# Token halves in the norms, and a new order of the second block's input units

## The chip, the cores and the metric

One core of a Trainium2 chip runs the whole program in one launch. The metric is the device time in microseconds of that core, the median of the runs. Engines: TensorE (PE), VectorE (DVE), ScalarE (ACT), GpSimd (POOL) and SyncE (SP), which issues the DMAs.

## The reference

Two transformer blocks follow each other, over 512 latent tokens (x) and 256 context tokens, width 1024, all in float32. The first has four layers: pooling mixer, neighbourhood attention, gated convolution, pooling mixer, and a last norm. Each layer is

```
h = rmsnorm(x, g) * (1 + scale) + shift        # scale, shift, gate from silu(c) @ ada_w
x = x + gate * mixer(h)
```

The second block has two layers; layer 0 updates the context too, layer 1 only x:

```
q, k, v, f, u, gv = split(modulate(rms_norm(x, g1)) @ w_in)
q, k = rope(rms_norm(q)), rope(rms_norm(k))    # 8 query heads, 2 key heads of 64
mix  = concat(attention(q, k, v), fourier_mix(f),
              gelu(u) * (w_s @ rms_norm(gelu(gv)) + b_s)) @ w_out
x = x + gt1 * mix
x = x + gt2 * (relu(modulate(rms_norm(x, g2)) @ w1) ** 2 @ w2)
```

fourier_mix is the real part of a two-dimensional transform over tokens and 64 features. The norms take the mean square over the 1024 features of each token; the head norms over 64.

## The kernel before

Activations lie transposed: features on the 128 partitions, in 8 tiles k, tokens along the free axis (T = TT = 768 with the context last, or TX = 512). The work is a list of steps made by plan(); each engine walks the same list and does its share of each step, so the list's order is every engine's queue. Semaphores are counters: act_done and dve_done count finished steps, turn_mm PE's finished turns. A step's a0 and d0 are the counts before it; ACT, as a rule, waits for all DVE steps ahead of it in the list (d0).

A unit is one output tile m of a projection: 8 weight tiles, each in three passes (high by high, high by low, low by high part of the float32 split), each pass one matmul of 512 columns and, for TT, one of 256. It writes one of two PSUM turns (PS); a turn is free when the step two turns before has been read (free_turn). Weights come one unit at a time: SP loads w_raw (two buffers), ACT rounds it to w_hi (round_unit, L1028), DVE makes w_lo (split_unit); three buffers of each, and unit w + 3 is made after unit w. Chunks of the conditioning matrices (ada_chunk, L1255) hang on the units on DVE, owed chunks being given to later units (with_ada).

A norm (norm(), ahead of each layer and each MLP) follows eight "xupd" units. In each, DVE updates x, ACT squares it into T1, DVE adds it to T4. After the eighth: "nstat" (PE sums T4 over partitions, L851; ACT takes the root; DVE the reciprocal and copies it over T3), "back" (PE transposes T3 into the score bank, L859), then eight "ntile" steps: DVE scales x by it into T1 or T2 (normed), ACT makes h_hi (L1088), DVE h_lo. The two first units after it are joined: PE interleaves them, the second two tiles behind, each tile as its H tile comes. keep_warm(n) runs n matmul pairs on constants into the score bank (L762): 8 before nstat, 2 before back, 8 before the joined pair.

In the second block the input units are, in order, sk (keys, TT), sq 0 to 3 (queries), v (TT), sf (Fourier inputs), su (gate), sgv (gate values). After the first half of a unit's tiles the previous unit's head norm stands in PE's list: "hnorm" (sums of squares, L867), keep_warm(2), "back", "rope" (a permutation, L871), then DVE and ACT finish q or k. After the last unit: "four1" (first transform, L973), the last gate value's hnorm, "gtrans" (transposes, L958), "spgate" (spatial gate, L965), "gsplit", each on its turn; then scores and "four2" (second transform, L982), whose tables DC and DS are loaded over the H tiles once the last input unit is done, and the softmax stages.

## Time and profile before

| | us |
|---|---|
| median of 3 runs (2890.43 to 2904.68) | 2893.8 |
| the profiled execution | 2895.74 |
| its span | 2893.9 |

Mean granted TensorE clock 0.975. From the page, busy time by engine and the clock in 40 slices (digits are tenths; a busy PE can be running dummies or waiting inside its pipeline):

```profile
PE 2757.8 (95%) x14298; PEld 2298.9 (79%) x14298; DVE 1696.1 (59%) x2615; ACT 937.7 (32%) x1432; POOL 156.1 (5%) x84
...
PEclk8999999999999999989999999999999999999999
```

Slices of 72 us are too coarse for the stages in question; the stage windows and timelines below cut the span where the step list does. Six norms are at 313, 802, 1045, 1657, 2215 and 2523 us; the second block's layers begin at 1258 and 2228 us.

### The profile page before, as it was taken

The numbers are of one execution on the slowest core, as the hardware profiler recorded it, in microseconds if no ns is written. First come the engines' busy times: TensorE is split into PE (matmuls) and PEld (weight loads), VectorE is DVE, ScalarE is ACT, GpSimd is POOL, SyncE is SP. The second block draws the span as 40 slices with busy tenths as digits, with TensorE's granted clock in tenths as the row PEclk, the third lists the DMA queues.
The fourth block names the chain that finished last, engine by engine and source line by source line (L and its number), as shares of the span: only waits on it lengthen the run. The fifth ranks groups of instructions, "written<-read, shape, count | busy, mean of one in ns | idle before, by whom it ended". The sixth has DMA issues, their size and how long they took to land. (4 is left out here: it accounts for less than half of the span.)

```text
span 2893.9 us, 36598 instructions
## 1 busy us (share of the span) xinstructions
PE 2757.8 (95%) x14298; PEld 2298.9 (79%) x14298; DVE 1696.1 (59%) x2615; ACT 937.7 (32%) x1432; POOL 156.1 (5%) x84
## 2 busy tenths in 40 slices
PE   7998999999999999989899999999999999999999
PEld 7887778888877877767677888888887768778887
DVE  4986666666577878765556664444235446454333
ACT  2322344444232233232355231313122345333222
POOL 0000000000000000000055000000000016100000
PEclk8999999999999999989999999999999999999999
DMA  5252334443345635322200323332112110122232
GB/s 215 72 172 97 108 123 143 138 136 134 109 155 181 195 106 171 118 78 83 93 1 1 110 95 130 118 124 70 62 59 63 55 63 1 59 80 95 95 95 95
DMA packets 88539, 296.32 MB, mean 102 GB/s; under 512 B 10288, under 2 KB 13360, under 8 KB 87856
## 3 DMA queue, kind: packets, MB, share of 16 engines
q1 hardware_dynamic: 88368, 293.98, 30.7%
q8 instruction: 114, 1.87, 0.3%
q14 instruction: 57, 0.47, 0.1%
HBM read 291.85 MB, written 2.10 MB: 102 GB/s over the span
## 5 line engine op out<-in xcount | busy, mean ns | idle before, releaser
L770 PE MATMUL turns<-h_hi,w_hi 128*128 128x512 f32 (+1 forms) x2480 | 788.2, 367 | 25.2 <-DVE h_lo L1244 13.5
L770 PE MATMUL turns<-h_hi,w_lo 128*128 128x512 f32 (+1 forms) x2480 | 773.1, 361 | 0.0
L770 PE MATMUL turns<-h_lo,w_hi 128*128 128x512 f32 (+1 forms) x2480 | 770.4, 360 | 0.0
L770 PEld LDWEIGHTS turns<-h_hi,w_hi 128*128 128x128 f32 x2480 | 418.6, 190 | 119.6 <-DVE h_lo L1244 27.8
L770 PEld LDWEIGHTS turns<-h_hi,w_lo 128*128 128x128 f32 x2480 | 416.1, 189 | 72.5
L770 PEld LDWEIGHTS turns<-h_lo,w_hi 128*128 128x128 f32 x2480 | 415.3, 189 | 71.1 <-issue 1.0
L1028 ACT ACTIVATE w_hi<-w_raw 128x1024 fp32r<-128x1024 f32 x300 | 315.4, 1051 | 373.8 <-PE turns L770 352.7
L1241 DVE TENSOR_TENSOR w_lo<-w_raw,w_hi 128x1024 fp32r<-128x1024 f32 x300 | 366.7, 1223 | 118.1 <-ACT w_hi L1028 117.7
L724 POOL TENSOR_SCALAR tmp<-tmp,softmax_stats 128x768 f32<-128x768 f32 (+1 forms) x80 | 155.9, 1951 | 2317.5 <-DVE softmax_stats L1477 2317.2
L1244 DVE SCALAR_TENSOR_TENSOR x_lat<-turns,modulation,x_lat 128x512 f32<-128x512 f32 x112 | 84.1, 750 | 317.5 <-PE turns L770 317.5
L770 PE MATMUL turns<-m_hi,w_lo 128*128 128x512 f32 (+1 forms) x768 | 232.9, 358 | 0.0
L770 PE MATMUL turns<-m_hi,w_hi 128*128 128x512 f32 (+1 forms) x768 | 232.9, 358 | 0.0
L770 PE MATMUL turns<-m_lo,w_hi 128*128 128x512 f32 (+1 forms) x768 | 231.8, 356 | 0.0
L1255 DVE CUSTOM_DVE_ANT_0 ada_raw<-ada_raw,cond_rows,ada_bias 128x1024 f32<-128x1024 f32 x176 | 225.2, 1280 | 2.9 <-DMA ada_raw<-in_adapack 2.1
L1241 DVE TENSOR_TENSOR tmp<-tmp 128x768 f32<-128x768 f32 (+7 forms) x96 | 79.9, 832 | 241.8 <-ACT m_hi L1211 241.0
L762 PE MATMUL scores<-dft,ones 128*128 128x256 f32 x500 | 142.3, 436 | 15.4 <-DMA pool_edges<-in_edge 15.4
L770 PEld LDWEIGHTS turns<-m_lo,w_hi 128*128 128x128 f32 x768 | 126.5, 188 | 23.4
L770 PEld LDWEIGHTS turns<-m_hi,w_hi 128*128 128x128 f32 x768 | 126.9, 188 | 22.9
L770 PEld LDWEIGHTS turns<-m_hi,w_lo 128*128 128x128 f32 x768 | 127.1, 188 | 21.9
L1210 ACT ACTIVATE tmp<-turns 128x768 f32<-128x768 f32 (+1 forms) x64 | 45.2, 706 | 287.0 <-PE turns L770 285.2
L762 PEld LDWEIGHTS scores<-dft,ones 128*128 128x128 f32 x500 | 106.0, 221 | 31.1 <-DMA pool_edges<-in_edge 15.4
L1182 ACT ACTIVATE tmp<-x_lat 128x512 f32<-128x512 f32 x56 | 35.4, 632 | 288.6 <-DVE x_ctx L1244 157.4
(217 smaller groups left out, 3353.8 us busy)
## 6 DMA issues: line engine op xcount, KB each, us to landing
w_raw<-in_wpack SPq DMA_DIRECT2D x300, 512.0 KB, 3.5
ada_raw<-in_adapack SPq DMA_DIRECT2D x176, 512.0 KB, 4.0
bias<-in_bias SPq DMA_DIRECT2D x64, 320.0 KB, 2.9
ada_first_a<-in_adapack SPq DMA_DIRECT2D x12, 512.0 KB, 8.7
x_lat<-in_xT SPq DMA_DIRECT2D x1, 2048.0 KB, 8.6
x_ctx<-in_ctxT SPq DMA_DIRECT2D x2, 1024.0 KB, 8.8
ada_first_b<-in_adapack SPq DMA_DIRECT2D x4, 512.0 KB, 14.7
cond_rows<-in_crow SPq DMA_DIRECT2D x4, 512.0 KB, 10.3
```

Of the source, the lines that this page charges most:

```text
L724: ins = pool.tensor_scalar(ex, ex, ST[:, x.eb, 6 + j:7 + j], None, ALU.mult)
L762: pe.matmul(dst, ONES[:], CS[:], start=True, stop=True)
L770: ins = pe.matmul(dst[:, lo:lo + sz], w, x[:, lo:lo + sz], start=first and n == 0, stop=last and n == 2)
L1028: act.activation(Wh[:, w % 3, :], RAW[:, w % 2, :], ACT.Copy).then_inc(w_rounded, 1)
L1182: ins = act.activation(T1[:, lo:lo + sz], xseg(lo, m), ACT.Square)
L1210: chain(act.activation(T1[:, 0:t], ps[:, 0:t], ACT.Relu))
L1241: return dve.tensor_tensor(dst, x, y, op)
L1244: return dve.scalar_tensor_tensor(out=dst, in0=x, scalar=c, in1=y, op0=op0, op1=op1)
L1255: ins = dve.tensor_tensor_reduce(dump, ADR[:, n % 2, :], CROW[:, c, :], 0.5, ADAB[:, sect, k:k + 1], ALU.mult, ALU.add, MOD[:, sect, c, k: ...
```

## The change

Six of the nine norms (all but the first, the one at the end of the first block and the one right after it) are cut by tokens. Of their eight updates the last three are made in two token parts (512 and 256 of 768, or 256 and 256 of 512): updates 5, 6, 7 of part a, then 5, 6, 7 of part b, each part with its own turn but the same weights. Statistics and H tiles of part a stand between the b updates, and the joined pair that follows runs over part a and then part b. These norms have no keep_warm. The sum of squares is a step of its own ("xsum"), after the weight split. Statistics of all norms lie in score bank 1 instead of a turn.

In the second block the order is sk, sq 0, v, sq 1 to 3, sgv, su, sf; they carry no conditioning chunks. Head norms stand inside the next unit, at given tiles, without keep_warm; every other unit has its own two temporaries (OWN). Gate transposes stand inside the last unit; after it first transform and spatial gate take turns. Weights are packed in the new order. The core of the diff:

```diff
+def parts_of(s):
+
+    if s.tok is not None:
+        return [(int(s.tok[0] >= TX), *s.tok)]
+    return [(0, 0, TX)] if s.T == TX else [(0, 0, TX), (1, TX, TC)]
+
+
+HALVES = {TX: ((0, TC), (TC, TC)), TT: ((0, TX), (TX, TC))}
...
+        if ev == "xupd" and a["nxT"]:
+            add("xsum", T=T, m=m)
...
+    def updated_norm(src, T, after, sect_u, g, sect, late=False):
+
+        for m in range(KT - 3):
+            full(src, "xupd", T, m, after=after if m == 0 else (), sect=sect_u, nxT=T, late=late and m == 0)
+        at = {}
+
+        def part(m, tok):
+            at[m, tok] = s = add("unit", src=src, ev="xupd", T=T, m=m, sect=sect_u, nxT=T, has_turn=True)
+            s.tok, s.twin = tok, at.get((m, a))
+            if tok is a:
+                s.twin = None
+                if m < KT - 1:
+                    with_ada(s)
+                else:
+                    owed[0] += 1
+            at[m, tok, "sum"] = x = add("xsum", T=T, m=m)
+            x.tok = tok
...
+        a, b = HALVES[T]
+        tiles = {a: [], b: []}
+        part(KT - 3, a)
+        part(KT - 2, a)
...
+        add("gain", g=g, T=T, sect=sect)
+        part(KT - 1, a)
+        part(KT - 3, b)
+        st = stat(a)
+        st.prepares = at[KT - 3, b]
+        back = spread(a, st)
+        tiles_of(a, back, range(1))
+        part(KT - 2, b)
+        at[KT - 2, b].inside = {4: [back]}
+        tiles_of(a, back, range(1, 2))
+        tiles[a][-1].prepares = at[KT - 2, b]
+        part(KT - 1, b)
+        tiles_of(a, back, range(2, 6))
+        st_b = stat(b)
+        tiles_of(a, back, range(6, KT))
+        tiles[a][-1].prepares = at[KT - 1, b]
+        back_b = spread(b, st_b)
+        tiles_of(b, back_b, range(KT))
+        back.inline = st_b.inline = back_b.inline = True
+        return (a, tiles[a]), (b, tiles[b]), {3: [st_b], 7: [back_b]}
...
-        add("nstat", T=T, g=g, sect=sect, has_turn=True)
+        add("nstat", T=T, g=g, sect=sect)
...
                 back.reader = add("gnorm", T=t, m=m, layer=L)
             else:
                 back.reader = add("rope", T=t, what=kind, m=m, layer=L, st=1)
...
+            back.reader.back, back.reader.own = back, u.own
+            hn.inline = back.inline = back.reader.inline = True
+            if kind == "sgv":
+                return [(4, hn), (7, back)], back.reader
+            return [(2, hn), (5, back), (5, back.reader)], back.reader
+
+        hn_of, gt, gsp, sf = {}, {}, {}, {}
+        sk = full("H", "sk", TT, 0, after=tiles, layer=L, what="sk", chunks=0)
+        sk.own = True
+        sq = full("H", "sq", T, 0, after=tiles, layer=L, what="sq", chunks=0)
+        join(sk, sq, split)
+        sk.first_tile = first_tile
+        todo = sk
+        for e, m, t in [("v", 0, TT)] + [("sq", m, T) for m in range(1, 4)] + [(e, m, T) for e in ("sgv", "su", "sf") for m in range(2)]:
+            inside = []
+            if e == "sq" and m == 1:
+                vt = add("vtrans")
+                vt.after, vt.inline = [v], True
+                inside.append((1, vt))
+            if todo is not None:
+                points, hn_of[todo.what, todo.m] = head_steps(todo)
+                inside += points
+            if e == "sf" and m == 1:
+                for n in range(2):
+                    gt[n] = add("gtrans", T=T, m=n, layer=L)
+                    gt[n].after, gt[n].inline = [hn_of["sgv", n]], True
+                    inside.append((3 + 3 * n, gt[n]))
+            u = full("H", e, t, m, layer=L, what=e, pair=0, chunks=0)
+            if e == "sq":
+                u.own, u.temps = m % 2 == 1, hn_of[("sk", 0) if m == 1 else ("sq", m - 2)]
+            for j, s in inside:
+                u.inside.setdefault(j, []).append(s)
+            todo = sq if e == "v" else u if e in ("sq", "sgv") else None
             if e == "v":
                 v = u
-            todo = u if e in ("sq", "sgv") else None
...
+        for m in range(2):
             for n0 in range(0, nts, 4):
-                add("spgate", T=T, m=m, n0=n0, nn=min(4, nts - n0), layer=L, has_turn=True).after = [gt[m]]
-
-        gtrans(0)
-        back = add("back", T=T)
-        four1()
-        back.reader = hn_of["sgv", 1] = add("gnorm", T=T, m=1, layer=L)
-        back.reader.back = back
-        spgate(0)
-        gtrans(1)
-        gsp[0] = add("gsplit", T=T, m=0)
-        while four:
-            four1()
-        spgate(1)
-        gsp[1] = add("gsplit", T=T, m=1)
+                nn = min(4, nts - n0)
+                ab.append(add("four1", m=m, n0=n0, nn=nn, has_turn=True, in_end=last_in))
+                ab[-1].after = [sf[m]]
+                add("spgate", T=T, m=m, n0=n0, nn=nn, layer=L, has_turn=True).after = [gt[m]]
+            gsp[m] = add("gsplit", T=T, m=m)
...
+        split = updated_norm("H", T, ready, sect + 2, 6 + L, sect + 3, late=True)
         for c in range(4):
-            hid = [full("H", "mlp", T, m, after=tiles if c == 0 and m < 2 else ()) for m in range(KT)]
+            hid = [full("H", "mlp", T, m) for m in range(KT)]
             if c == 0:
-                join(hid[0], hid[1])
+                join(hid[0], hid[1], split)
+            if c == 3 and L == 0:
+                split = updated_norm("M", T, hid, sect + 5, 5, SECT0[5])
+                continue
...
+            def head_step(s):
+
+                if s.tok is not None:
+                    norm_step(s)
+                elif s.kind == "back":
+                    wait_steps(s.after)
+                    free_scores(0, s)
+                    for n in range(s.T // P):
+                        ins = pe.transpose(SP_[:, 0, n * P:n * P + P], T3[:, n * P:n * P + P], IDN[:])
+                    ins.then_inc(score_mm[0], 1)
...
+            def pair_by_parts(u, v):
+
+                for tok, tiles in u.split:
+                    both = [x for x in (u, v) if tok[0] < x.T]
+                    lag = 2 * (len(both) - 1)
+                    for j in range(KT + lag):
+                        if tok[0] == 0:
+                            run_inside(u, j)
+                        for x, k in zip(both, (j, j - lag)):
+                            if tok[0] == 0 and k == 0:
+                                pe.wait_ge(w_split, x.w + 1)
+                                free_turn(x)
+                            if 0 <= k < KT:
+                                if x is both[0]:
+                                    wait_steps(tiles[k:k + 1])
+                                ends = 0 if x is v and v.T < u.T else 1 + (v.T < u.T)
+                                tile(x, k, k == 0, k == KT - 1, [(None, *tok)], ends if sum(tok) == x.T else 0)
...
+                if s.split:
+                    pair_by_parts(s, v)
+                    return
...
                 elif s.kind == "nstat":
-                    if s.g != 0:
+                    if s.tok is None and s.g != 0:
                         keep_warm(26 if s.g == 4 else 8)
-                    pe.wait_ge(dve_done, s.d0)
-                    free_turn(s)
-
-                    for n in range(s.T // P):
-                        ins = pe.matmul(PS[:, b, n:n + 1], T4[:, n * P:n * P + P], ONES[:, 0:1], start=True, stop=True)
-                    ins.then_inc(turn_mm, 1)
+                    if s.tok is None:
+                        pe.wait_ge(dve_done, s.d0)
+                    else:
+                        wait_steps(s.after)
+                    free_scores(1, s)
+                    stat_sums(s)
                 elif s.kind == "back":
-
-                    keep_warm(2)
-                    pe.wait_ge(dve_done, s.d0)
+                    if s.tok is None:
+                        keep_warm(2)
+                        pe.wait_ge(dve_done, s.d0)
+                    else:
+                        wait_steps(s.after)
                     free_scores(0, s)
-                    for n in range(s.T // P):
-                        ins = pe.transpose(SP_[:, 0, n * P:n * P + P], T3[:, n * P:n * P + P], IDN[:])
-                    ins.then_inc(score_mm[0], 1)
+                    scale_back(s)
...
-                    pe.wait_ge(act_done, s.a0)
+                    wait_steps(s.after)
...
-                if prev is not None and prev.kind == "unit" and turn_of_w[prev.w] == prev.turn:
+                if prev is not None and prev.kind == "unit" and prev.twin is None and turn_of_w[prev.w] == prev.turn:
                     round_unit(prev.w + 3)
+                if prev is not None and prev.prepares is not None:
+                    round_unit(prev.prepares.w + 3)
...
+                if s.temps is not None:
+                    act.wait_ge(dve_done, s.temps.d1)
...
+                elif s.kind == "xsum":
+                    for _, lo, sz in parts_of(s):
+                        ins = act.activation(T1[:, lo:lo + sz], xseg(lo, s.m, sz), ACT.Square)
+                    give(ins)
...
+                elif s.kind == "xsum":
+                    take()
+                    done(sum_squares(s.m, [x[1:] for x in parts_of(s)]))
...
-                if s.kind == "unit" and turn_of_w[s.w] == s.turn:
+                if s.kind == "unit" and s.twin is None and turn_of_w[s.w] == s.turn:
                     split_unit(s.w + 3)
+                if s.prepares is not None:
+                    split_unit(s.prepares.w + 3)
...
-        cols(w, 640)
-        for m in range(6):
+            if m == 0:
+                cols(w, 640)
+        for m in (4, 5, 2, 3, 0, 1):
```

## Rows read from the trace of the kernel before

**Rows 1.** The page: its first line.

```profile
span 2893.9 us, 36598 instructions
```

**Rows 2.** Busy time by stage, eight units each; columns in the second line.

```profile
core 0: us, PE busy (x) PEld busy (x) DVE busy (x) ACT busy (x) POOL busy (x), PEclk, DMA share, GB/s
2012.40:2079.80 67.40, 67.40 (x387) 59.06 (x386) 19.02 (x24) 10.04 (x10) 0.00 (x0) 1.00 0.20 63
2625.50:2669.10 43.60, 43.60 (x194) 36.11 (x193) 19.63 (x23) 16.32 (x22) 0.00 (x0) 1.00 0.26 85
```

**Rows 3.** Busy time by stage, same columns, the six norms with following units.

```profile
313.20:352.20 39.00, 34.23 (x150) 27.03 (x149) 26.84 (x48) 14.71 (x26) 0.00 (x0) 0.91 0.18 60
802.40:831.40 29.00, 28.24 (x120) 22.08 (x119) 20.49 (x31) 10.24 (x14) 0.00 (x0) 0.94 0.27 93
1044.90:1123.40 78.50, 72.88 (x312) 58.64 (x310) 65.64 (x107) 25.00 (x34) 0.00 (x0) 0.96 0.30 98
1656.50:1742.00 85.50, 82.09 (x440) 69.83 (x439) 56.64 (x84) 29.39 (x41) 0.00 (x0) 0.96 0.30 103
2215.20:2248.00 32.80, 27.67 (x129) 21.07 (x128) 22.11 (x41) 13.13 (x23) 0.00 (x0) 0.95 0.14 45
2523.50:2580.80 57.30, 54.95 (x242) 43.37 (x241) 32.54 (x43) 22.88 (x32) 0.00 (x0) 1.00 0.23 73
```

**Rows 4.** Busy time by stage, same columns, second block, layers 0 and 1.

```profile
1277.90:1409.30 131.40, 114.11 (x630) 95.88 (x629) 76.41 (x113) 34.33 (x44) 0.00 (x0) 0.92 0.28 88
1409.30:1439.60 30.30, 22.99 (x102) 17.93 (x101) 16.46 (x34) 11.55 (x15) 0.00 (x0) 0.89 0.34 122
2248.00:2339.30 91.30, 82.93 (x381) 66.32 (x381) 42.20 (x61) 30.58 (x45) 0.00 (x0) 0.94 0.20 64
2339.30:2360.10 20.80, 16.56 (x76) 12.78 (x74) 9.80 (x22) 9.28 (x13) 0.00 (x0) 0.92 0.36 126
```

**Rows 5.** Timeline of DVE, norm before layer 1: start, us, operation, idle before.

```profile
2215.33 0.75 DVE L1244 SCALAR_TENSOR_TENSOR x_lat<-turns,modulation,x_lat 128x512 f32<-128x512 f32 x1 [4.02 <-PE turns L770]
...
2217.55 1.03 DVE L1241 TENSOR_TENSOR tmp<-tmp,tmp 128x512 f32<-128x512 f32 x2 [1.08 <-ACT tmp L1182]
2218.50 1.23 DVE L1241 TENSOR_TENSOR w_lo<-w_raw,w_hi 128x1024 fp32r<-128x1024 f32 x1
...
2228.14 0.75 DVE L1244 SCALAR_TENSOR_TENSOR tmp<-x_lat,gain_cols,scores 128x512 f32<-128x512 f32 x1
2228.80 0.47 DVE L1244 SCALAR_TENSOR_TENSOR tmp<-x_ctx,gain_cols,scores 128x256 f32<-128x256 f32 x1
2229.23 1.15 DVE L1244 SCALAR_TENSOR_TENSOR h_lo<-tmp,modulation,h_hi 128x512 fp32r<-128x512 f32 x2
2230.48 0.75 DVE L1244 SCALAR_TENSOR_TENSOR tmp<-x_lat,gain_cols,scores 128x512 f32<-128x512 f32 x1
```

**Rows 6.** Timeline of PE, value products of 256 columns, six starts apart.

```profile
2475.76 0.28 PE L950 MATMUL turns<-pt_hi,v_lo 128*128 128x256 f32 x1
...
2476.48 0.28 PE L950 MATMUL turns<-pt_hi,v_lo 128*128 128x256 f32 x1
```

**Rows 7.** Timeline of PE and ACT, k's head norm in layer 1.

```profile
2247.79 1.39 PE L867 MATMUL scores<-head_ones,tmp 128*128 128x2 f32 x12
2249.04 1.11 PE L762 MATMUL scores<-dft,ones 128*128 128x256 f32 x4
2250.69 0.85 PE L859 MATMUL scores<-ident,tmp 128*128 128x128 f32 x6 [0.54 <-DVE tmp L1414]
2251.37 1.02 PE L871 MATMUL scores<-tmp,rope_swap 128*128 128x512 f32 x2
...
2255.82 0.84 ACT L1108 ACTIVATE sk_hi<-tmp 128x768 fp32r<-128x768 f32 x1 [6.24 <-DVE tmp L1244]
```

**Rows 8.** Timeline of PE and DVE, first gate product of layer 1.

```profile
2350.06 1.89 PE L965 MATMUL turns<-w_spatial,tmp 128*128 128x256 f32 x8
...
2352.24 2.40 DVE L1241 TENSOR_TENSOR tmp<-turns,b_spatial 64x128 f32<-64x128 f32 x8
```

**Rows 9.** DMA issues of 2310 to 2380 us: KB, us to landing.

```profile
dft_sin<-in_dft_sin SPq DMA_DIRECT2D x1, 1024.0 KB, 7.6
```

274 lines of the change are left out of this document (149 added, 125 removed).

## The prediction

> **What bounds the kernel now.** I read the page first, then busy time by stage, then the timelines around the stages where TensorE (PE) is not full. The span is 2893.9 us [rows 1]. In the projections and MLPs PE is 100% busy at the full clock: eight units over 768 tokens take 67.4 us, 8.43 us each, and eight over 512 tokens 43.6 us, 5.45 us each [rows 2]. A unit is 24 weight tiles, each with one matmul of 512 columns or one of 512 and one of 256. So PE sets the end, and time is to be had only where it idles, is kept warm with dummy matmuls, or runs at the lower clock. PE's busy share hides that, since dummies count as busy. I therefore take the elapsed time of a stretch less the units in it.
>
> The reader is to see three kinds of stretch. First, six norms between an update and the next projections [rows 3]. The units in the windows are, in order of the rows: q, k, g (two of 5.45 and one of 8.43); three of 5.45; eleven of 5.45; eight of 8.43; one of each; eight of 5.45. That leaves 39.0-19.3 = 19.7, 29.0-16.4 = 12.6, 78.5-60.0 = 18.5, 85.5-67.4 = 18.1, 32.8-13.9 = 18.9 and 57.3-43.6 = 13.7 us, together 101.5 us, with granted clocks of 0.91 to 1.00. Second, the input units of the second block after their first pair: 131.4 us in its first layer, 91.3 in its second [rows 4]. Units alone would be 10 x 8.43 = 84.3 and 8.43 + 9 x 5.45 = 57.5 us. Third, what lies between the last input unit and the second Fourier transform: 30.3 and 20.8 us [rows 4], in which no large matmul runs.
>
> **The norms.** Before, everything waits for the last update: sum, square root, transpose back, then eight H tiles on VectorE (DVE), and DVE makes one in 2.34 us (2228.14 to 2230.48) [rows 5] while the pair wants one in 2.1. Now the last three updates are cut into token parts a and b, and part a's statistics and first tiles run while PE does part b. The same DVE operations remain, most in two pieces, and from here on DVE sets the end of the stretch. I count DVE's queue from the end of the last a part on PE (time 0).
>
> For 768 tokens (a 512, b 256): part a's sum is ready at 2.4. The row of the update shows 0.75 us for 512 columns, then a gap of 1.08 for ScalarE (ACT), then the sum [rows 5]. After it DVE has three b updates with sums (an estimate of 1.5 each, half of what the same chain takes for 768 columns, 2215.33 to 2218.50), 4.5; three weight splits of 1.23, 3.7; eight a tiles of twice 0.66, 10.6; eight b tiles of twice 0.43, 6.8 [rows 5]; two reciprocals and copies, an estimate of 1.3; about 2 of waits on ACT and PE between pieces. That is 28.9, so the last b tile is there at 31.3 and the pair ends at about 32.5 (31.5 where only one of the pair has a part b). With three a parts of 5.45 before time 0 the whole is 48.9 us, against 42.2 us of units (three updates and a pair of 8.43): 6.7 us lost. With one unit of 5.45 in the pair it is 47.9 against 39.2, 8.7 lost. The first case is the norm before the MLP of layer 0 (18.1 before, gain 11.4); the second the norm before the neighbourhood attention (gain 11.0) and before layer 1 (gain 10.2).
>
> For 512 tokens (256 and 256) the matmuls themselves are cut. Does a matmul of 256 columns with its own weights cost half? The value products show six starts in 0.72 us, 0.12 us each, at full clock [rows 6]: 24 take 2.9 us, so a unit in two parts costs 5.8 rather than 5.45, and five such units cost 1.8 us more per norm. DVE: part a's sum at 1.6, then 4.5 + 3.7 + 16 x 0.85 + 1.0 + 2.5 = 25.3, the pair ends at 28.4, with three parts before 37.2 to 37.4, against 27.3 of units: 10.1 lost. Before the last MLP 13.7 goes to 10.1 (gain 3.6). The other two also carry chunks of the conditioning matrices on DVE; DVE is busy 65.6 of 78.5 us in the third window [rows 3], and I leave them what they lose beyond that: gains 1.5 and 3.5. Six norms: 41 us.
>
> From it comes the clock. In time 0 to 10.6 PE has b parts, but the third a tile comes only at 15.9 (DVE has splits and b updates ahead of it), so PE stands still for some 3.5 us right after the pair has begun, with no dummies to cover it; both calls of them go. Before, clocks of 0.91 to 0.96 stood in windows with idle times of that size [rows 3]. A stretch at half clock costs what it hides of matmuls; I take 1.3 us a norm, 8 in all (0 to 20). Norms: 33 us.
>
> The page "TensorE: Matmul & The Clock Gate" of the Trainium skill (Part 3, The mechanism) says a weight load overlaps a running matmul only when their row groups differ. All of ours use the full array, so by it each added load would be paid. The trace differs: rows 6 have a load for every 0.12 us start. By the page's figure of 107 ns for 128 columns, 360 added loads would cost 38 us, an estimate by that page.
>
> **The input units of the second block.** The order becomes k, q0, v, q1 to q3, gate values, gate, Fourier inputs, and each head's norm runs inside the next unit: sum of squares after two tiles, transposes and rope permutation after five. Removed: the dummies (1.11 us a head [rows 7]) and the waits. Kept on PE: 1.39, 0.85 and about 0.5 us a head [rows 7], some 2.5 for 768 tokens and 2.05 for 512. New waits: the sum of squares needs ACT's evacuation of the unit, queued behind the previous head's rope on DVE and ACT. After the permutation come four DVE operations and a tail (3.2 us), ACT's copy 0.84 [rows 7], an evacuation of two such operations, 1.7, against three tiles, a permutation and two tiles on PE (5.7): 0.5 us short in layer 0, 1.3 in layer 1, where units are shorter. V's transposes after one tile wait 1.6 and 2.0 by the same count. The sums of the gate values wait for a longer evacuation (square, two DVE steps, tanh, two DVE steps, each 0.6 to 0.96 us by width): 3.9 + 1.3 and 4.2 + 1.4, estimates. V and the two gate transposes cost 0.85 (0.6) each. Layer 0: 84.3 + 5 x 2.5 + 2 x 2.1 + 3 x 0.85 + waits (1.6 + 3 x 0.5 + 5.2) = 112. Layer 1: 57.5 + 2.5 + 4 x 2.05 + 2 x 1.6 + 2.0 + waits (2.0 + 3 x 1.3 + 5.6) = 85. Gains 19 and 6. Conditioning chunks leave this stage for the MLPs, where DVE is busy 19.0 of 67.4 us [rows 2] and hides them.
>
> **Between inputs and transform.** What was serial (gate values' norm, both transposes, dummies) is gone from here; four (eight) steps of PE remain, 1.89 us or half of it each. Ruling is the PSUM turn: the second gate product waits until DVE has read the first, 2.40 us [rows 8]. Layer 1: 1.75 x 4 + 0.5 of wait + 1.1 of scores = 8.7 us. Layer 0 by the same rule, with the first gate's split in DVE's way: 15. Gains 12.1 and 15.3. Next late is the table of the transform, landing 7.6 us after the last input unit [rows 9], just under 8.7, so not late; were it, a microsecond.
>
> **Small costs.** In the three norms that stay whole, the statistics now lie in the bank that the two dummies before the transposes write, so these wait for DVE and follow it instead of running beside it: 1.11 us each [rows 7], 3 in all. New half-clock pieces at the waits of 4 us: 5.
>
> Sum: 33 + 25 + 27 - 3 - 5 = 77 us. The profiled execution was timed at 2895.7 (span 2893.9), the median is 2893.8, 1.9 less. 2895.7 - 77 = 2818.7 and by the median 2816.8: I say 2817.
>
> **Rivals.** (1) DVE sets the norms later than counted: each piece of the queue hands over to ACT and back, and if every handover costs a further 0.3 us (some 25 per norm) the norms' gain goes and 2850 is left. For it: the 1.08 gap in rows 5. Against: tiles ran back to back at 2.34, ACT hidden. (2) The stalls are too short to drop the clock and unit starts catch up: the 13 us for the clock are not paid, and 2804 results. For it: the last window ran at 1.00 [rows 3]. (3) Weight loads show in narrow matmuls: 360 loads (three norms, five units, 24 tiles) at 0.153 us, 59.06 us of loading over 386 [rows 2], would be 55 us, 2872; rows 6 speak against it. It is the rule of the Trainium skill named above. (4) Slower: without dummies the clock falls in each norm and stays down through the input units. These stretches hold about 260 and 200 us; each microsecond at half clock costs half of one, so 77 us of gain are gone at 154 us more of it, a third of the stretches, and at 210 us the time is 2922. For it: the windows before had dummies and still 0.91. Against: PE in them is now 80 to 90% busy with wide matmuls, as at 0.95 in the fifth window. (5) The order doesn't do what it says: part a's tiles come after part b anyway and only the second block gains, 2847; the queue above gives tile 0 at 9 us, before PE's b parts end at 10.6.
>
> **How the numbers follow.** Forecast 0.53, (1) 0.15, (2) 0.18, (3) 0.03, (4) 0.04, (5) 0.07. The range must hold the first three: from 2795, where (2) meets no added wait, to 2856. A measurement here tells about 0.5%, 14 us. Faster by that holds for all but (3) in part and (4): 0.94; same 0.02; slower 0.04.
>
> **What would show it.** After the change: the six windows with 6 to 15 us beyond their units; PE idle for 3 to 4 us once in each, waiting for an H tile of DVE; k to last input 112 and 85 us; first Fourier step to transform 15 and 9 us; value-product spacing 0.12 us in the cut units. Wrong it would be if the granted clock in these windows falls under 0.9, if w_lo or the raw weights end a wait, or if the softmax stages grow by what was gained ahead of them.

## The result, and the profile after

| | us | ratio to before, 95% interval |
|---|---|---|
| before, median (2890.43 to 2904.68) | 2895.23 | |
| after, median of 4 runs (2856.14 to 2874.52) | 2865.32 | 0.9893 [0.9852, 0.9934] |
| after, the profiled execution | 2866.62, span 2864.8 | |

The change is faster, by 30 us or 1.1%, where 77 us were forecast: the sign is right, and the time lies 9 us outside the range. First the six norms, as busy time by stage of the kernel after, with the columns of rows 2 (elapsed us, busy us of PE, PEld, DVE, ACT and POOL with their counts, granted clock, DMA). The stretches end where those of rows 3 end, but begin with the first a part, so they hold three update units more:

```profile
290.00:349.90 59.90, 52.75 (x257) 43.22 (x256) 44.20 (x76) 22.78 (x38) 0.00 (x0) 0.91 0.23 75
782.80:828.30 45.50, 40.46 (x280) 37.03 (x278) 34.89 (x69) 19.01 (x34) 0.00 (x0) 0.96 0.32 106
1025.00:1117.90 92.90, 84.92 (x473) 73.16 (x471) 81.70 (x149) 32.05 (x51) 0.00 (x0) 0.98 0.34 109
1610.60:1722.10 111.50, 104.25 (x559) 89.29 (x558) 81.34 (x123) 37.78 (x53) 0.00 (x0) 0.94 0.31 104
2170.00:2221.20 51.20, 45.38 (x236) 37.44 (x234) 33.44 (x58) 17.91 (x31) 0.00 (x0) 0.96 0.19 60
2475.10:2551.60 76.50, 69.88 (x398) 61.54 (x397) 44.38 (x76) 31.93 (x52) 0.00 (x0) 0.93 0.23 70
```

Take the units away (three more of 8.43 or 5.45 us each than in rows 3: 44.6, 32.7, 76.3, 92.7, 39.2 and 59.9) and 15.3, 12.8, 16.6, 18.8, 12.0 and 16.6 us remain, together 92 instead of 101.5. Forecast were 60 before the clock's 8. The clock is the column to look at: 0.91, 0.96, 0.98, 0.94, 0.96, 0.93, where the cut norms were meant to be fuller than the whole ones, and the last window had stood at 1.00 [rows 3].

Now the input units after their first pair and what lies between them and the transform, first layer 0, then layer 1 (before: 131.4, 30.3, 91.3, 20.8 us [rows 4]), and the softmax stage of layer 0, before and after, whose program is the same in both:

```profile
1272.70:1395.40 122.70, 114.41 (x635) 98.54 (x635) 52.66 (x72) 39.78 (x52) 0.00 (x0) 0.92 0.16 48
1395.40:1414.90 19.50, 15.25 (x57) 11.22 (x55) 10.83 (x28) 5.81 (x7) 0.00 (x0) 0.83 0.49 189
2221.20:2318.20 97.00, 83.67 (x379) 67.04 (x379) 45.97 (x68) 37.30 (x55) 0.00 (x0) 0.90 0.20 60
2318.20:2327.80 9.60, 8.59 (x39) 6.73 (x38) 4.98 (x12) 4.22 (x5) 0.00 (x0) 1.00 0.70 274
```

```profile
1439.60:1589.70 150.10, 141.85 (x842) 112.03 (x843) 91.14 (x153) 78.86 (x164) 85.25 (x48) 0.97 0.00 1
```

```profile
1414.90:1568.40 153.50, 144.79 (x843) 113.50 (x843) 89.24 (x149) 78.79 (x164) 85.12 (x48) 0.94 0.00 1
```

The last pair is a scale for the clock. The same work takes 3.4 us longer at 0.94 than at 0.97. A stretch's length times (1 - clock) is the most that the clock can have cost it (4.5 and 9.2 us here, 4.7 apart for 3.4 measured): time at half clock in which PE only waits costs nothing. The inputs of layer 1 have become longer, 97.0 for 91.3, although dummies and waits are gone from them; 0.10 x 97.0 = 9.7 us is the clock's share at most.

All 14 kernels have the program of these two softmax stages, and the traces give the price of the clock. In layer 0 the stage took 148.0 us with 7.5 us of it at half clock (the clock records know two levels, full and half), 151.7 with 13.7 and 154.0 with 18.1; a straight line through the 14 gives 0.51 us for each us at half clock. In layer 1 it took 119.7 to 120.1 us in the eight traces with none, and 124.3 or 124.4 in the three with 10.2.

The waits of TensorE in the kernel after, longest totals first (engine and line, awaited, us in total, times, longest):

```profile
PE turns L839 <- DVE h_lo L1396: 33.1, 34, 3.1
...
PE scores L870 <- DVE tmp L1396: 10.0, 4, 3.6
...
PE turns L839 <- DVE m_lo L1393: 5.0, 2, 3.0
```

The first is the H tiles, 34 waits (19 of 13.5 us together in the kernel before), where one deep one in each cut norm had been counted. The second is the waits of the gate values' sums. The third was in no term of the forecast's sum: PE waits behind a pair for the pair's own evacuation.

One norm closely, that before the MLP of layer 0. Its last a part ends where the first matmul of part b starts, at 1628.75. Timeline of VectorE (start, us, operation; in brackets the idle time before it and what ended it):

```profile
1630.66 0.69 DVE L1393 TENSOR_TENSOR tmp<-tmp,tmp 128x512 f32<-128x512 f32 x1 [0.84 <-ACT tmp L1237]
...
1652.44 1.22 DVE L1393 TENSOR_TENSOR w_lo<-w_raw,w_hi 128x1024 fp32r<-128x1024 f32 x1
1655.42 0.87 DVE L1396 SCALAR_TENSOR_TENSOR tmp<-x_ctx,gain_cols,scores 128x256 f32<-128x256 f32 x2 [1.76 <-PE scores L903]
...
1659.03 0.48 DVE L1396 SCALAR_TENSOR_TENSOR tmp<-x_ctx,gain_cols,scores 128x256 f32<-128x256 f32 x1
1659.43 0.48 DVE L1396 SCALAR_TENSOR_TENSOR h_lo<-tmp,modulation,h_hi 128x256 fp32r<-128x256 f32 x1
1660.01 0.48 DVE L1396 SCALAR_TENSOR_TENSOR tmp<-x_ctx,gain_cols,scores 128x256 f32<-128x256 f32 x1
...
1663.14 0.48 DVE L1396 SCALAR_TENSOR_TENSOR h_lo<-tmp,modulation,h_hi 128x256 fp32r<-128x256 f32 x1 [0.28 <-ACT h_hi L1243]
1666.24 0.96 DVE L1393 TENSOR_TENSOR tmp<-tmp 128x768 f32<-128x768 f32 x1 [2.61 <-ACT m_hi L1363]
```

and of TensorE:

```profile
1628.75 0.28 PE L839 MATMUL turns<-h_hi,w_hi 128*128 128x256 f32 x1
...
1632.64 0.28 PE L839 MATMUL turns<-h_lo,w_hi 128*128 128x256 f32 x1
1632.76 0.28 PE L839 MATMUL turns<-h_hi,w_lo 128*128 128x256 f32 x1
...
1640.72 0.50 PE L839 MATMUL turns<-h_hi,w_hi 128*128 128x512 f32 x1 [0.84 <-DVE h_lo L1396]
...
1644.77 0.79 PE L839 MATMUL turns<-h_hi,w_hi 128*128 128x512 f32 x1 [3.08 <-DVE h_lo L1396]
1645.36 0.63 PE L839 MATMUL turns<-h_lo,w_hi 128*128 128x512 f32 x1
1645.79 0.63 PE L839 MATMUL turns<-h_hi,w_lo 128*128 128x512 f32 x1
...
1652.18 0.39 PE L839 MATMUL turns<-h_hi,w_hi 128*128 128x512 f32 x1
1652.41 0.39 PE L839 MATMUL turns<-h_lo,w_hi 128*128 128x512 f32 x1
...
1665.09 0.28 PE L839 MATMUL turns<-h_hi,w_lo 128*128 128x256 f32 x1
1668.34 0.98 PE L839 MATMUL turns<-h_hi,w_hi 128*128 128x512 f32 x2 [2.96 <-DVE m_lo L1393]
1669.11 0.85 PE L839 MATMUL turns<-h_lo,w_hi 128*128 128x512 f32 x2
1669.76 0.84 PE L839 MATMUL turns<-h_hi,w_lo 128*128 128x512 f32 x2
```

The third tile comes 16.0 us after the last a part (forecast 15.9), and PE waits 3.08 us for it. After this wait a matmul of 512 columns starts every 0.43 us, from 1652.18 every 0.23: first the lower level of the clock, then the full one. Because of that the transposes of part b's statistics (L903), which stand behind part a's tiles on PE, come late, and VectorE, the engine that is to set the end, idles 1.76 us. It then makes a b tile in 0.98 us (1659.03 to 1660.01). Behind the pair PE waits 2.96 us, and again goes on at the lower level: a tile's pair of matmuls (512 and 256 columns) starts every 0.65 us (1669.11 to 1669.76), where at the full clock it is 0.35 (8.43 us for 24).

### The profile page after: what moved, and what is told of

Read it like the earlier page. It is cut to its first block and busy times, and to the rows that moved or that the text cites. A ratio compares the mean times of both kernels' runs of the same rounds, so it can differ in the third digit from the quotient of the medians.

```text
span 2864.8 us, 36946 instructions
## 1 busy us (share of the span) xinstructions
PE 2720.0 (95%) x14362; PEld 2286.7 (80%) x14362; DVE 1708.9 (60%) x2693; ACT 949.5 (33%) x1471; POOL 155.9 (5%) x84
## 5 line engine op out<-in xcount | busy, mean ns | idle before, releaser
L839 PE MATMUL turns<-h_hi,w_hi 128*128 128x512 f32 (+1 forms) x2552 | 828.9, 368 | 52.1 <-DVE h_lo L1396 33.1
L839 PE MATMUL turns<-h_hi,w_lo 128*128 128x512 f32 (+1 forms) x2552 | 811.3, 361 | 0.0
L839 PE MATMUL turns<-h_lo,w_hi 128*128 128x512 f32 (+1 forms) x2552 | 807.9, 360 | 0.0
L839 PEld LDWEIGHTS turns<-h_hi,w_hi 128*128 128x128 f32 x2552 | 446.3, 194 | 142.5 <-DVE h_lo L1396 45.0
L839 PEld LDWEIGHTS turns<-h_hi,w_lo 128*128 128x128 f32 x2552 | 445.0, 193 | 71.1
L839 PEld LDWEIGHTS turns<-h_lo,w_hi 128*128 128x128 f32 x2552 | 444.0, 193 | 70.1 <-issue 1.0
L1396 DVE SCALAR_TENSOR_TENSOR x_lat<-turns,modulation,x_lat 128x512 f32<-128x512 f32 (+1 forms) x121 | 86.1, 711 | 314.7 <-PE turns L839 312.0
L1407 DVE CUSTOM_DVE_ANT_0 ada_acc<-ada_raw,cond_rows,ada_bias 128x1024 f32<-128x1024 f32 x88 | 112.6, 1280 | 1.8
L1243 ACT ACTIVATE h_hi<-tmp,modulation 128x256 fp32r<-128x256 f32 (+1 forms) x128 | 70.9, 572 | 86.7 <-DVE tmp L1396 86.7
L1393 DVE TENSOR_TENSOR pt_lo<-turns,pt_hi 128x768 fp32r<-128x768 f32 (+1 forms) x72 | 66.6, 926 | 42.9 <-ACT pt_hi L1277 42.5
```

The lines of the kernel that those rows point to most:

```text
L839: ins = pe.matmul(dst[:, lo:lo + sz], w, x[:, lo:lo + sz], start=first and n == 0, stop=last and n == 2)
L1243: ins = act.activation(Hh[:, s.k, lo:lo + sz], src[:, lo:lo + sz], ACT.Identity, bias=MOD[:, s.sect, c, s.k:s.k + 1], scale=1.0)
L1393: return dve.tensor_tensor(dst, x, y, op)
L1396: return dve.scalar_tensor_tensor(out=dst, in0=x, scalar=c, in1=y, op0=op0, op1=op1)
L1407: ins = dve.tensor_tensor_reduce(dump, ADR[:, n % 2, :], CROW[:, c, :], 0.5, ADAB[:, sect, k:k + 1], ALU.mult, ALU.add, MOD[:, sect, c, k: ...
```

## Experiments

The kernels below are changes of the kernel after or of one another. The row "after" of the result (2865.32, 0.9893 [0.9852, 0.9934]) is the one to compare with. The intervals are 9 to 24 us wide, so the times alone don't tell kernels apart that lie a few us from each other. "Dummies" are the pairs of small matmuls that `keep_warm` issues. Some of the quoted expectations were written against a theory by name: the clock theory (waits without dummies cost clock in what follows), theory E (VectorE's chain of tiles sets the end of a cut norm) and theory F (the handover of PSUM turns behind the pair does).

| kernel | median us | ratio to before, 95% |
|---|---|---|
| heads only | 2874.40 | 0.9926 [0.9901, 0.9951] |
| norms only | 2889.63 | 0.9979 [0.9964, 0.9994] |
| dummies in norms | 2858.36 | 0.9874 [0.9850, 0.9898] |
| dummies in heads | 2859.77 | 0.9880 [0.9854, 0.9905] |
| dummies in both | 2842.26 | 0.9827 [0.9801, 0.9852] |
| shorter b tiles | 2845.84 | 0.9841 [0.9813, 0.9869] |
| part b earlier | 2861.34 | 0.9878 [0.9852, 0.9905] |
| 512-token norms whole | 2848.14 | 0.9842 [0.9821, 0.9863] |
| value order | 2845.27 | 0.9816 [0.9790, 0.9842] |
| late split | 2837.91 | 0.9799 [0.9778, 0.9820] |
| both orders | 2834.15 | 0.9787 [0.9756, 0.9817] |
| no dummies behind pairs | 2840.00 | 0.9799 [0.9758, 0.9841] |

Where single stages are compared, they are cut at the same instructions, with the time at half clock, summed from the trace's clock records, in brackets. One profiled execution of each kernel stands behind a column:

```
stage (us, half clock)          before        after         in norms      in both       late split    both orders   no tail dummies
norm, neighbourhood, layer 0    107.8 ( 6.8)  102.6 (10.2)  100.9 ( 0.0)  101.3 ( 3.4)  101.6 ( 0.0)  101.7 ( 0.0)  101.4 ( 6.8)
norm of the second window       241.4 (10.2)  242.2 (13.7)  239.9 ( 6.8)  240.1 ( 6.8)  239.2 ( 6.8)  239.0 ( 6.8)  238.5 ( 6.8)
norm of the third window        156.6 (10.2)  151.1 ( 3.4)  155.0 (10.2)  154.9 (10.2)  152.5 ( 3.4)  153.5 ( 6.8)  152.0 ( 3.4)
first pair and inputs, layer 0  151.5 (20.5)  142.3 (20.5)  142.8 (20.5)  138.6 ( 6.8)  138.2 ( 6.8)  135.6 ( 3.4)  138.2 (10.2)
to the transform, layer 0        30.3 ( 6.8)   19.5 ( 6.6)   19.0 ( 3.2)   18.1 ( 3.4)   19.5 ( 6.1)   17.6 ( 0.0)   19.5 ( 6.1)
norm before the MLP, layer 0    152.2 ( 6.8)  153.7 (17.1)  148.3 ( 3.4)  148.1 ( 3.1)  146.9 ( 3.4)  147.1 ( 3.4)  146.2 ( 3.4)
norm and inputs, layer 1        191.7 (13.6)  190.4 (23.9)  188.8 (17.1)  188.8 (17.1)  184.8 (10.2)  182.3 ( 6.8)  187.4 (20.5)
norm before the last MLP        100.9 ( 0.0)  103.7 (10.2)  101.5 ( 3.4)  101.5 ( 0.0)  100.0 ( 0.0)  100.0 ( 0.0)  100.1 ( 0.0)
half clock of these and the transform's in layer 1
                                 78.5         105.5          64.7          50.9          36.8          27.3          57.3
```

**Heads only, norms only: how the gain divides.** The first leaves all norms whole:

```diff
+        for m in range(KT):
+            full(src, "xupd", T, m, after=after if m == 0 else (), sect=sect_u, nxT=T, late=late and m == 0)
+        return norm(T, g, sect)
```

> The second block's new order alone: all nine norms whole, as before the change, with their dummies. My sum for the prediction had 33 us from the six cut norms and 47 from the second block: by it this kernel takes 2895 - 44 = 2851. Theory A (read from the two traces): the stages of the second block's inputs and transforms gained 29 us and the cut norms with their neighbours next to nothing, so this kernel takes 2865 to 2870, like the changed one. Theory B (the norms gained, the second block gave it back in its softmax stages): near 2890.

The second keeps the cut norms and has the second block as before: order, head norms with their dummies, gate transposes, weight layout.

```diff
-                    scores_in(s.m, s)
-                    done(act.activation(GT[s.m][:, 0:t // P, :], SP_[:, s.m, 0:t]
+                    done(act.activation(GT[s.m][:, 0:t // P, :], ps[:, 0:t]
...
-        for m in (4, 5, 2, 3, 0, 1):
+        for m in range(6):
```

> The cut norms alone: the second block's input units, head norms and gate in the order of before. By my sum 2895 - 33 + 3 = 2865. Theory A: 2888 to 2893, since by the traces the six norms gained some 6 us together. If the two parts disturb each other, x1 and x2 gain more together than the change does (30 us).

22 and 6 us of gain by the medians and ratios, together what the whole change brings: the parts add up. The cut norms, forecast at 33, bring 2 to 10 us alone by the interval. The heads, forecast at 44 with the stretch to the transform, bring half, and 2874.4 is above the 2865 to 2870 that I had expected from the traces. So the miss is in both parts. That fits a cause that both share, but doesn't show one.

**Dummies into the waits: is it the clock?** Six pairs stand ahead of the third H tile of part a, five behind the pair, in each cut norm. Nothing else changes in the program.

```diff
+                        if tok[0] == 0 and j == 2:
+                            keep_warm(6)
...
                     pair_by_parts(s, v)
+                    keep_warm(5)
```

> The changed kernel with 6 pairs of dummies where the joined pair waits for its third H tile, and 5 pairs where the next unit waits for its PSUM turn. Theory C (the clock eats the norms' gain: PE catches up at half clock after each wait): the half clock behind these waits goes, and the time falls by 8 to 15 us to 2850 to 2857. Theory D (VectorE's queue and the evacuation behind it set the end of these stretches, whatever the clock): granted clock rises, the time stays within 4 us of the changed kernel, and VectorE's last tile comes at the same distance from the last a part as now (35 us in the norm before the MLP of layer 0).

```diff
                 elif s.kind == "hnorm":
+                    if s.what != "sk":
+                        keep_warm((6 if s.m == 0 else 3) if s.what == "sgv" else 1 if s.T == TT else 2)
                     wait_steps(s.after)
```

> The changed kernel with dummies of about the length of the waits ahead of each head norm (1 or 2 pairs, 6 and 3 for the gate values). Theory C: half-clock stretches of 3.4 us behind these waits (I count 24 us in layer 0 and 14 us in layer 1 up to the last input unit) go, each gives back half, up to 19 us in all: 2846 to 2855. Theory D': the clock falls for the many small matmuls of head norm and transposes, dummies or not: no change, 2863 to 2870.

The medians are 7.0 and 5.6 us under the kernel after, both just short of the range of the clock theory (2850 to 2857 and 2846 to 2855), and the intervals overlap that of the kernel after: the times alone don't decide. The stages do. The norm before the MLP of layer 0 takes 148.3 us with dummies, with 3.4 of them at half clock. In the three kernels that have this norm cut and no dummies in it (after, norms only, dummies in heads) it takes 149.5 to 153.7, with 10.2 to 17.1. Its pair ends 34.8 or 35.1 us after the last a part in the four kernels that have these dummies and no other edit of this norm, and 36.6 in the kernel after (37.1 with norms only, 35.4 with dummies in the heads alone); VectorE's last tile is there at 33.0 instead of 34.9, so the low clock on PE had held VectorE up too, against theory D. The inputs of layer 0 fall from 142.3 to 137.9 us, and their half clock from 20.5 to 6.8.

In layer 1 the second kernel gained nothing (192.1 for 190.4): its two pairs of dummies stand longer than the wait they were to fill, and a head takes 9.8 us there, where one at the full clock without them takes 9.3. Both together, with dummies only at the gate values there:

```diff
+                    if s.what == "sgv":
+                        keep_warm(6 if s.m == 0 else 3)
+                    elif s.what == "sq" and s.T == TT:
+                        keep_warm(1)
```

> The dummies of x3 (norm waits) and of x4 together, the latter only where they fit into a wait: one pair for the queries of layer 0, 6 and 3 pairs for the gate values, none for the queries of layer 1, where x4 lost 0.5 us a head to them. If the two regain different half-clock stretches the gains add: 2864 less 6 to 8 (x3) less 5 to 7 (x4), 2849 to 2853. If one stretch only moves to the next place (the clock falls elsewhere), it stays at 2856 to 2860.

2842.3 us, 23 under the kernel after by the medians and 19 by the ratios, and the executions don't overlap (2840.3 to 2851.7, 2856.1 to 2874.5). This is more than the two parts together, 12.6, and under the expected range, and the traces say why: 9.1 of the 26.3 us between the two profiled executions lie ahead of the first unit, where the programs are the same. The stages in the table are 14.1 us shorter together. The third window's is an exception, 3.8 us longer with dummies in the norms. Still, work that computes nothing, put where PE waited anyway, makes the program faster, so the waits themselves weren't all that cost; what followed them at half clock did too.

The traces of the 14 kernels repeat this. The wait of 2.6 to 3.1 us for the third H tile is followed, within 8 us, by 2.9 to 6.7 us at half clock in all 18 cut norms without dummies in it (after, norms only, dummies in heads), and by none in all 51 with them. In layer 0 the waits of the last three queries, 0.4 to 0.5 us, are followed within 6 us by 3.3 or 3.4 us of it in 11 of 12 cases without a pair of dummies, and by none in 24 with one. At the first query, where no wait of this kind stood, the dummies changed nothing clear: some half clock follows in two of four cases without them and in five of eight with them.

One head of layer 0 shows it closely. Kernel after (timeline of PE; then windows with the columns above):

```profile
1300.54 1.50 PE L870 MATMUL scores<-head_ones,gmlp_v 128*128 128x2 f32 x12 [0.52 <-ACT gmlp_v L1352]
...
1303.49 0.84 PE L839 MATMUL turns<-h_hi,w_hi 128*128 128x512 f32 x2
1304.13 0.84 PE L839 MATMUL turns<-h_lo,w_hi 128*128 128x512 f32 x2
...
1314.08 1.50 PE L870 MATMUL scores<-head_ones,tmp 128*128 128x2 f32 x12 [0.50 <-ACT tmp L1352]
```

```profile
1300.50:1304.00 3.50, 3.46 (x20) 3.12 (x21) 1.92 (x3) 1.21 (x2) 0.00 (x0) 0.78 0.17 14
1304.00:1307.80 3.80, 3.80 (x20) 3.19 (x19) 0.00 (x0) 0.00 (x0) 0.00 (x0) 0.75 0.34 129
1307.80:1314.00 6.20, 5.78 (x32) 4.64 (x30) 3.96 (x6) 2.31 (x4) 0.00 (x0) 1.00 0.00 0
```

The same head with one pair of dummies in that wait (from the kernel with both orders, below), timeline and window:

```profile
1296.31 0.70 PE L831 MATMUL scores<-dft,ones 128*128 128x256 f32 x2
1296.85 1.46 PE L874 MATMUL scores<-head_ones,gmlp_v 128*128 128x2 f32 x12
...
1299.30 0.51 PE L839 MATMUL turns<-h_hi,w_hi 128*128 128x512 f32 x2
1299.65 0.51 PE L839 MATMUL turns<-h_lo,w_hi 128*128 128x512 f32 x2
...
1308.81 1.35 PE L874 MATMUL scores<-head_ones,tmp 128*128 128x2 f32 x11
```

```profile
1296.80:1320.70 23.90, 23.85 (x141) 19.92 (x140) 11.77 (x18) 7.07 (x11) 0.00 (x0) 1.00 0.15 45
```

From one head to the next 13.54 us (1300.54 to 1314.08) against 11.96 (1296.85 to 1308.81). A tile's pair of matmuls starts every 0.64 us after the wait, every 0.35 with the dummies. The granted clock after a wait of 0.52 us is 0.78 and 0.75, two levels mixed; with 0.70 us of dummies there it is 1.00 throughout. The 1.58 us between the heads are a little under half of the 3.4 us at half clock.

**Shorter b tiles: does VectorE's chain set the end?** From the kernel with dummies in the norms. The low part of H is made for 8 of part b's 256 columns, the other columns are left out; the chain of VectorE is shorter by this, and PE's work is unchanged.

```diff
+                        if s.tok is not None and lo:
+                            sz = 8
                         ins = stt(Hl[:, s.k, lo:lo + sz], ...
```

> x3 with the low part of part b's H tiles made for 8 of its 256 columns only (the other columns keep what an earlier norm left; this leaves work out, for its time alone). Theory E (VectorE's chain of part b tiles, one per 0.98 us by the trace against 0.85 in my sum, sets the end of each cut norm): 8 tiles x 6 norms x 0.3 to 0.4 us off VectorE's chain, so 12 to 19 us faster than x3, 2840 to 2846. Theory F (PE or the PSUM turn behind the pair sets it): under 5 us, 2854 to 2858.

12.5 us less than with whole b tiles (2858.4), in five norm stages 2.3, 0.7, 3.8, 1.9 and 1.9 less (the third with 10.2 us less at half clock). In the norm before the MLP the pair ends at 33.0 us instead of 34.8. Theory E holds: of what VectorE saves in part b's chain, at most 8 x 0.48 = 3.8 us a norm, about half comes out at the end.

**Part b earlier.** If tiles come late, part b could start sooner, with the pair's first unit through part b before its second:

```diff
-        return (a, tiles[a]), (b, tiles[b]), {3: [st_b], 7: [back_b]}
+        return (a, tiles[a]), (b, tiles[b]), {3: [st_b], 6: [back_b]}
...
-                    lag = 2 * (len(both) - 1)
+                    lag = (2 if tok[0] == 0 else KT) * (len(both) - 1)
```

> x5 with part b's transposes one tile earlier (after six tiles instead of seven) and, in part b, the first unit of the pair run to its end before the second, so that its PSUM turn is handed over earlier. Theory F (turn handover behind the pair, 2 to 3 us in each of six norms): it hides the second unit's 3 us under the first one's evacuation and the third unit starts 0.7 to 1.5 us earlier in each, 4 to 8 us faster than x5. Theory E: at most 1 us a norm from the transposes, 0 to 4 us.

This failed: 2861.3 us, 19 more than its base. The second unit now stands behind the first as a tail that no VectorE work covers, and the pair of the norm before the MLP ends 36.6 us after the last a part, for 34.8 in the base. Five norm stages are 9.9 us longer together. In the three norms of 512 tokens PE now also rests 1.35 us inside part b, without dummies, and 1.1 to 6.2 us at half clock follow within 8 us. The profiled execution, its fastest, is 10.4 us longer than the base's; of the rest of the 19 no trace tells.

**The 512-token norms whole.** Three of the six cut norms had small forecast gains (3.6, 1.5, 3.5). The base is the kernel with dummies in both:

```diff
+        if T == TX:
+            for m in range(KT):
+                full(src, "xupd", T, m, after=after if m == 0 else (), sect=sect_u, nxT=T, late=late and m == 0)
+            return norm(T, g, sect)
```

> x5 with the three norms of 512 tokens left whole, as before the change. By my sum the cut gained 8.6 us in them (1.5, 3.5, 3.6): 8 us slower than x5. Theory G (the cut costs there what it gains: 1.8 us of narrow matmuls, the handover, VectorE's pieces): within 3 us of x5.

6 us more by the medians, but the intervals overlap, and the stages don't bear it out: against the base the second window's stage is 2.5 longer and the last norm 1.8, the third window's 2.5 shorter and the mixing unit behind it 1.9. This stays open: cutting these three is worth between nothing and 6 us.

**Two orders.** The units go gate, gate values, gate, gate values, Fourier inputs, so that another kind of evacuation follows the last query:

```diff
-... for e in ("sgv", "su", "sf") for m in range(2)]
+... for es in (("su", "sgv"), ("sf",)) for m in range(2) for e in es]
...
-        for m in (4, 5, 2, 3, 0, 1):
+        for m in (2, 4, 3, 5, 0, 1):
```

> The kernel with small matmuls in both norms and heads, with one thing changed: the second block's units come in the order gate, gate values, gate, gate values, Fourier inputs (su0, sgv0, su1, sgv1, sf0, sf1) instead of gate values first. Theory: the first gate value's wait of 3.3 us (layer 0) and 3.6 us (layer 1) is its evacuation queued behind the last query's rotary work on VectorE and ScalarE; with a gate's evacuation there, which needs no such chain, the wait falls to the 1.4 to 1.6 us of the second gate value, so about 4 us less in all: 2836 to 2840 us. Rival: the wait is the handover of the new kind of unit itself, wherever it stands: no change, 2842 us, with the same two waits at their new places.

And the last weight split moves from before part b's tiles to behind them:

```diff
-        tiles[a][-1].prepares = at[KT - 1, b]
...
+        tiles[b][-1].prepares = at[KT - 1, b]
-        return (a, tiles[a]), (b, tiles[b]), {3: [st_b], 7: [back_b]}
+        return (a, tiles[a]), (b, tiles[b]), {3: [st_b], 6: [back_b]}
```

> The kernel with small matmuls in both norms and heads, with VectorE's order in part b of the cut norms changed: the last weight split stands behind the b tiles' normalization instead of before it, and part b's second half begins after six tiles. Theory that VectorE's chain of tiles sets the end of the pair (1.23 us of split ahead of it in each of six norms): 5 to 7 us less, 2835 to 2838 us. Rival, that the pair's end is set by the handover of accumulators behind it: 0 to 2 us, 2840 to 2842 us.

The value order isn't told from its base by the medians (2845.3 and 2842.3); its input stages are 2.7 and 2.1 us shorter (layer 0, and norm and inputs of layer 1), each with 3.4 us less at half clock, while the first stages of the program, which it doesn't touch, happened to be 13 us longer. The time that PE still waited behind the six pairs of dummies for the first gate values, 0.74 us in layer 0 and 1.05 in layer 1, is gone, as the theory has it; how much shorter the whole wait is can't be seen under the dummies. The late split has 2837.9, and its interval overlaps that of its base too; the norm stages decide. They give 0.9 to 2.4 us less (the largest with 6.8 us less at half clock), but for the first of them. In the norm before the MLP the pair now ends 33.6 us after the last a part (in all three kernels with this edit), 1.2 sooner, as a term of 1.23 in VectorE's chain should. The edit also puts part b's transposes one tile earlier; the two aren't told apart.

> Both of the last edits together: the late weight split with part b's second half after six tiles, and the units in the order gate, gate values, gate, gate values, Fourier inputs, with small matmuls in both norms and heads. If the two gains are separate (7 us in the norms, 4 to 5 us in the inputs), about 2833 us, and the stages keep what each run showed alone: inputs of layer 0 about 136, the normalization before layer 1 with its inputs 4 us under the one of the kernel with small matmuls in both. Rival: the order's gain was variation of the clock between runs: 2838 us, as with the late split alone.

2834.2, the fastest of all, 61 us under before and 31 under the kernel after. Its norm before the MLP and its inputs of layer 0 after the pair, beside the rows of after above:

```profile
1592.80:1697.80 105.00, 102.59 (x577) 88.14 (x576) 81.21 (x123) 37.67 (x53) 0.00 (x0) 1.00 0.33 109
1265.50:1381.50 116.00, 112.81 (x662) 96.78 (x661) 52.74 (x72) 39.79 (x52) 0.00 (x0) 0.99 0.17 50
1381.50:1399.00 17.50, 12.34 (x56) 9.51 (x54) 9.88 (x27) 5.81 (x7) 0.00 (x0) 1.00 0.54 211
```

105.0 for 111.5 us at clock 1.00 for 0.94. Of the 6.5 us between them 1.2 are the late split's; the other 5.3 stay under the clock's bound of 0.06 x 111.5 = 6.7. With the late split alone the time was 3.8 us longer, within the spread of both.

**No dummies behind the pairs.**

```diff
                     pair_by_parts(s, v)
-                    keep_warm(5)
```

> As both orders together, but the five pairs of small matmuls behind the pair's last part are left out, so that TensorE stands still there until VectorE has evacuated the pair. Theory, that any rest of some microseconds beside this work costs clock in what follows: 3.1 us of rest in each of six norms, up to 3.4 us of half clock behind each and so 1.7 us lost for each, 2833 plus 10: 2843 us. Rival, that only the rests inside part b cost clock, which lie among short runs of work: 2833 us, or a little less.

Its executions run from 2832.5 to 2847.9 us and the intervals overlap, so the times don't decide. In five norms the stage is shorter, by 0.3, 0.5, 1.5 and 0.9 us, or the same, but a stage also holds half clock that comes and goes elsewhere in it. Behind the rest itself the trace is clear. In the norm before the MLP:

```profile
1651.53 0.51 PE L839 MATMUL turns<-h_lo,w_hi 128*128 128x512 f32 x2
1651.88 0.51 PE L839 MATMUL turns<-h_hi,w_lo 128*128 128x512 f32 x2
...
1653.19 0.84 PE L839 MATMUL turns<-h_hi,w_lo 128*128 128x512 f32 x2
1653.83 0.84 PE L839 MATMUL turns<-h_hi,w_hi 128*128 128x512 f32 x2
```

The spacing goes from 0.35 to 0.64 us. The two units behind the rest take 18.2 us, with 3.4 at half clock, for 16.6 to 16.9 in four kernels with the dummies (both, value order, late split, both orders); the unit behind the pair of layer 1 takes 12.8 for 11.2 or 11.3. In the second and third windows and the last norm no half clock follows the rest, and the units take as long as with dummies (16.2 for 16.2 to 16.4). In the neighbourhood norm 5.8 us follow it. So the rests behind the pairs, 1.5 to 3.0 us, are followed by half clock in three norms of six, for 1.3 to 1.6 us in the two where it can be priced; with dummies there, none follows in 45 of 45. A gain of the whole program from them isn't shown. That the inputs (2.6 and 5.1 us) and both softmax stages are longer in this execution lies for the most part at places whose program is the same as that of both orders.

## Why the prediction was right and wrong

| | forecast gain, us | measured in the profiled run |
|---|---|---|
| six norms with their clock (41 - 8) | 33 | 12.5 |
| input units after the pair, with their clock (25 - 5) | 20 | 3.0 |
| between inputs and transform | 27 | 22.0 |
| dummies behind VectorE in whole norms | -3 | not told apart |
| softmax stages | 0 | -3.8 |
| all else | 0 | -4.6 |
| sum | 77 | 29 |

The norms' 12.5 us are from the stages cut at the same instructions (5.3, -0.9, 5.5, -1.5, 7.0, -2.8); the windows above give 9.4, mostly since before the third of them 2.4 us more passed in the kernel before. Of "all else" 3.1 us lie before the first unit, which started at 76.0 and 79.1; among the kernels here it started between 69.5 and 79.7 with the same program up to there, so that isn't the change's.

**The step that failed first is the clock.** It stood in the sum at 13 us (1.3 us a norm, 5 in the heads), and rests in every cut norm and ahead of the head norms brought much more of it. The sum took what a window was longer than its units as gone, half clock of before with it, and then charged 1.3 us a norm and 5 in the heads for the new waits. At most 23 us are the clock's in the six windows of after (59.9 x 0.09 + 45.5 x 0.04 + 92.9 x 0.02 + 111.5 x 0.06 + 51.2 x 0.04 + 76.5 x 0.07), 19.5 in the inputs and 3.3 in what follows in layer 0: 46, where 13 stood in the sum. The softmax of layer 0 adds 3.4. The lower side is measured: with dummies in the waits and nothing else changed the stages compared are 14.1 us shorter, though much of the clock remained (50.9 us at half clock in them, for 105.5). The medians say 23 and the ratios 19, with what lies ahead of the first unit in them. So 14 us of the miss of 48 are shown to be the clock, up to 36 may be (46 - 13 + 3.4). Time at half clock in the stages compared fell from 105.5 to 50.9, 36.8 and 27.3 us while the median fell from 2865 to 2842, 2838 and 2834; the last two steps are edits of order as well, so only the first is the clock's alone. Half clock costs less here than the half of it that the softmax stages show, since part of it lies over waits.

The rest of the miss is work and waits that were sized too small or left out, some 30 us by an estimate from the rows below: 2.3 us of VectorE's chain in each of six norms (14), the rests behind the pairs (11.8 together in the last kernel, less 1.9 that stood in two places before), half a us of permutation in each of six heads over 768 tokens (3), and the steps before the transform (3.4). In the norms this part is the larger: with dummies the five norm stages of the table without input units are 13.0 us shorter than before, where 31.0 were forecast for these five before the clock's charge.

Rival (4), the clock against the change, was the right mechanism with the wrong size: priced only as a turn of sign at 154 us, when its partial form belonged in the main sum. Rival (2), that waits of this length don't drop the clock, is refuted: half clock followed all 18 of the long ones.

**VectorE's chain: right in kind, short by 3.6 us.** In the norm before the MLP part a's sum was ready 2.6 us after the last a part (forecast 2.4); the third tile at 16.0 (15.9); the last b tile at 34.9 (31.3). Of the 3.6 us, 1.0 is the tile, 0.98 instead of 0.85 us eight times, 1.76 the idle time before the first b tile, which the low clock on PE made, and the rest small pieces. The pair ended at 36.6 instead of 32.5; with dummies, at full clock, it ended at 34.8, and the last tile came at 33.0. Rival (1) has its mechanism in this, at some 2 us a norm rather than the 7 that would have made it 2850.

**A wait that wasn't in the sum.** With the b parts of both units at the end, the pair finishes both turns close together, and the next unit waits for one to be evacuated: 2.96 us before the MLP of layer 0, 2.00 before the last (0.86 and 1.03 in the kernel before). Behind all six pairs the rests are 1.5 to 3.0 us in the kernel without dummies there. The forecast ended the norm with the pair.

**The heads: the waits right, the work a little short.** Waits of 0.52, 0.50 and 0.51 us were forecast at 0.5, the gate values' 3.33 and 1.44 at 3.9 and 1.3, V's 1.99 at 1.6; in layer 1 V's 2.34 at 2.0, the queries' 1.31, 1.30 and 1.31 at 1.3, and 3.62 and 1.59 at 4.2 and 1.4. But even at full clock a head takes 11.96 us with 0.53 of it in the wait's place, for 11.4 forecast: the rope permutation costs PE 1.0 us (1.02 in rows 7), where I had taken half. Ten units became 122.7 for 112 and 97.0 for 85, and at most 9.8 and 9.7 us of these are the clock's. The kernel with both orders has 116.0 at 0.99.

**Between inputs and transform**, 9.6 for 8.7 us and 19.5 for 15. At clock 1.00 the second is 17.5, so 2 us are the clock's and 2.5 were missing in the count of its eight steps.

**The checks named ahead.** The single wait of 3 to 4 us for an H tile is there (3.08). Matmuls of 256 columns with their own weights start every 0.12 us in the cut units (1632.64, 1632.76), so rival (3) falls. The Trainium skill's rule in "TensorE: Matmul & The Clock Gate" (Part 3, The mechanism), that a load overlaps a running matmul only when their row groups differ, doesn't fit these 0.12 us; the same section also names loads into a background weight buffer, and no run here tells whether these are such. No wait for w_lo stands among the long ones. The granted clock of the norms stayed above 0.9, my sign for "wrong", and yet the clock was a cause: the threshold was set too low, as 0.06 of a window of 111.5 us is 6.7 us. The softmax stage grew, as the last sign says, by 3.4. Rival (5) is refuted: the first tile of part a was ready 8.8 us after the last a part, before PE's b parts ended at 10.3 (forecast 9 and 10.6).

What isn't settled: why half clock falls on one stage in one run and not in the next (the third window's stage, 3.4 us at half clock after and 10.2 with dummies in the norms), and so the exact split of the miss. 17 us lie between the fastest kernel and the forecast; the wait behind the pairs, 3.0 and 2.0 us in the two MLP norms, the b tiles and the permutation are the terms known to be in it, but no run measured their sum.
